# High and low rows side by side in one matmul of 512 columns, in expert jobs of 256 columns

## What is computed

```
def moe(h, router, wg, wu, wd):
    ...
    xs = xf[tok]
    hid = jax.nn.silu(lax.ragged_dot(xs, wg, sizes)) * lax.ragged_dot(xs, wu, sizes)
    ys = lax.ragged_dot(hid, wd, sizes) * gate.reshape(-1)[order][:, None].astype(h.dtype)
    return jnp.zeros_like(xf).at[tok].add(ys).reshape(B, S, D)
```

## Time and profile before

| | |
|---|---|
| Time, median of 3 runs | 4846.22 us (4843.46 to 4847.0) |
| Profiled execution | 4847.46 us, of it 4845.9 us span |
| TensorE matmuls busy in the span | 4269.3 us (88%) |
| VectorE busy in the span | 2434.7 us (50%) |
| ScalarE busy in the span | 1658.1 us (34%) |
| Expert jobs | from about 2480 us to 4778 us |
| VectorE busy in a job of 384 columns, 2733 to 3076 us | 183.07 of 343 us |
| Weights of a tile, 1 MB, from issue to landing | 4.9 us in the median |
| Granted TensorE clock, mean over the span | 0.937 of full |

### The profile page before, as it was taken

One profiled execution on the slowest core, in us unless ns is written; L12 is line 12 of the kernel. 1 busy time (PEld: TensorE's weight loads), 2 busy tenths in 40 slices (PEclk: granted clock), 3 DMA queues, 4 the chain that ended last, 5 costly groups with the idle time before them and its releaser, 6 DMA issues. The chain is left out here.

```text
span 4845.9 us, 66553 instructions
## 1 busy us (share of the span) xinstructions
PE 4269.3 (88%) x23962; PEld 3696.7 (76%) x23963; DVE 2434.7 (50%) x3287; ACT 1658.1 (34%) x2153; POOL 523.0 (11%) x905
## 2 busy tenths in 40 slices
PE   5799999995965688887559999999999999998994
PEld 4688888884864555555459999899999999998993
DVE  3344444452223576652346555566666665554554
ACT  1222222222224466662134333344444444232321
POOL 0000000001122354430120000100000000000001
PEclk9899999996987799998579999999999999999997
DMA  3422232215334211102445433455555554333334
GB/s 115 159 97 95 104 121 95 104 61 179 110 90 155 72 62 51 42 28 98 163 172 184 179 119 128 170 191 198 191 198 191 197 191 178 122 130 136 130 130 178
DMA packets 176461, 643.57 MB, mean 133 GB/s; under 512 B 29936, under 2 KB 68336, under 8 KB 136819
## 3 DMA queue, kind: packets, MB, share of 16 engines
q1 hardware_dynamic: 144452, 540.31, 31.1%
q0 software_dynamic: 20800, 71.87, 3.9%
q10 hardware_dynamic: 11040, 29.36, 1.7%
HBM read 556.88 MB, written 84.59 MB: 132 GB/s over the span
## 5 line engine op out<-in xcount | busy, mean ns | idle before, releaser
L345 PE MATMUL moe_ps<-moe_ht_hi,moe_gu_hi 128*128 128x256 f32 (+1 forms) x3584 | 1085.9, 303 | 24.2 <-issue 19.8
L347 PE MATMUL moe_ps<-moe_ht_hi,moe_gu_lo 128*128 128x256 f32 (+1 forms) x3584 | 1085.0, 303 | 0.0
L346 PE MATMUL moe_ps<-moe_ht_lo,moe_gu_hi 128*128 128x256 f32 (+1 forms) x3584 | 1084.8, 303 | 0.0
L345 PEld LDWEIGHTS moe_ps<-moe_ht_hi,moe_gu_hi 128*128 128x128 f32 x3584 | 683.7, 191 | 30.7 <-issue 25.9
L346 PEld LDWEIGHTS moe_ps<-moe_ht_lo,moe_gu_hi 128*128 128x128 f32 x3584 | 683.8, 191 | 3.8
L347 PEld LDWEIGHTS moe_ps<-moe_ht_hi,moe_gu_lo 128*128 128x128 f32 x3584 | 683.6, 191 | 0.0
L190 ACT CAST moe_gu_hi<-moe_gu_raw 128x2048 fp32r<-128x2048 f32 x226 | 431.4, 1909 | 642.8 <-PE moe_ps L347 520.6
L256 DVE TENSOR_TENSOR moe_gu_lo<-moe_gu_raw,moe_gu_hi 128x2048 fp32r<-128x2048 f32 x226 | 517.3, 2289 | 241.2 <-ACT moe_gu_hi L190 241.2
L286 DVE TENSOR_TENSOR moe_yacc<-moe_yacc,moe_ps 128x512 f32<-128x512 f32 x532 | 362.0, 688 | 378.1 <-PE moe_ps L365 377.4
L363 PE MATMUL moe_ps<-moe_wd_hi,moe_hid_hi 128*128 128x512 f32 x1064 | 415.9, 391 | 0.0
L364 PE MATMUL moe_ps<-moe_wd_lo,moe_hid_hi 128*128 128x512 f32 x1064 | 415.5, 390 | 0.0
(11 more groups left out here) (280 smaller groups left out, 6706.3 us busy)
## 6 DMA issues: line engine op xcount, KB each, us to landing
moe_gu_raw<-in_moe_wgu SPq DMA_DIRECT2D x226, 1024.0 KB, 4.9
moe_wd_raw<-in_moe_wd SPq DMA_DIRECT2D x112, 1024.0 KB
ffn_gu_raw<-in_ffn_wgu SPq DMA_DIRECT2D x58, 1024.0 KB
ffn_wd_raw<-in_ffn_wd SPq DMA_DIRECT2D x28, 1024.0 KB, 5.2
y_moe<-zeros SPq DMA_DIRECT2D x32, 512.0 KB, 3.0
kvq_raw<-in_w_kvq SPq DMA_DIRECT2D x12, 1024.0 KB
qkv<-kvq_o POOLq DMA_DIRECT2D x40, 256.0 KB, 4.9
qt<-heads_qt POOLq DMA_DIRECT2D x16, 512.0 KB, 3.4
```

The costliest lines, as they stand in the source:

```text
L345: pe.matmul(out[:, 0:W], gu_hi[s][:, half, k, :], ht_hi[:, k, 0:W], start=(k == 0), stop=False)
L346: pe.matmul(out[:, 0:W], gu_hi[s][:, half, k, :], ht_lo[:, k, 0:W], start=False, stop=False)
L347: last = pe.matmul(out[:, 0:W], gu_lo[s][:, half, k, :], ht_hi[:, k, 0:W], start=False, stop=(k == KT - 1))
```

## The change

Only jobs of 256 columns change. `ht_hi` and `ht_lo` become two halves of one tile `ht`. A step k of gate or up now has two matmuls in place of three: the high weights run once over 512 columns, the 256 high token columns and the 256 low ones side by side, into the left and the right half of the bank; the low weights run over the 256 high columns into the left half. The value of gate or up is then the sum of both halves. VectorE makes it with a reduction over pairs that lie 256 columns apart: gate into `act_gate`, up into `hid`, each signalled. ScalarE's silu now reads `act_gate`, in SBUF, and waits for the gate sum instead of for TensorE; VectorE's product reads `hid` and waits for silu and for its own up sum. In all other widths VectorE only counts the two new semaphores on.

```
@@ swiglu_jobs @@
-        ht_hi = sb("ht_hi", [P, KT, CAP * P], F32R)
-        ht_lo = sb("ht_lo", [P, KT, CAP * P], F32R)
+        ht = sb("ht", [P, 2, KT, CAP * P], F32R)
+        ht_hi, ht_lo = ht[:, 0, :, :], ht[:, 1, :, :]
...
+        s_gate_sum, s_up_sum = sem("gate_sum"), sem("up_sum")
+
+        def paired(W):
+
+            return 2 * W <= 512
...
                     def silu(N, s):
+                        if paired(W):
+                            act.wait_ge(s_gate_sum, N + 1)
+                            act.activation(act_gate[s][:, 0:W], act_gate[s][:, 0:W], ACT.Silu).then_inc(s_silu, 1)
+                            return
...
                     def product(N, s):
+                        if paired(W):
+                            dve.wait_ge(s_gate, N + 1)
+                            dve.tensor_reduce(act_gate[s][:, 0:W], gate_ps[s][:, 0:2 * W].rearrange("p (a n) -> p n a", a=2),
+                                              AX.X, ALU.add).then_inc(s_gate_sum, 1)
+                            dve.wait_ge(s_gu, N + 3)
+                            dve.tensor_reduce(hid[s][:, 0:W], up_ps[s][:, 0:2 * W].rearrange("p (a n) -> p n a", a=2),
+                                              AX.X, ALU.add).then_inc(s_up_sum, 1)
+                            dve.wait_ge(s_silu, N + 1)
+                            dve.wait_ge(s_up_sum, N + 1)
+                            dve.tensor_tensor(hid[s][:, 0:W], act_gate[s][:, 0:W], hid[s][:, 0:W], ALU.mult).then_inc(s_hid, 1)
+                            return
+                        dve.sem_inc(s_gate_sum, 1)
+                        dve.sem_inc(s_up_sum, 1)
...
                             for k in range(KT):
+                                if paired(W):
+                                    pe.matmul(out[:, 0:2 * W].rearrange("p (a n) -> p a n", a=2), gu_hi[s][:, half, k, :], ht[:, :, k, 0:W],
+                                              start=(k == 0), stop=False)
+                                    last = pe.matmul(out[:, 0:W], gu_lo[s][:, half, k, :], ht_hi[:, k, 0:W],
+                                                     start=False, stop=(k == KT - 1))
+                                    continue
```

## The result

| | before | changed |
|---|---|---|
| Time, median | 4846.6 us (4843.5 to 4853.5) | 4929.4 us (4925.6 to 4937.4) |
| Ratio, 95% interval | | 1.0171 (1.0153 to 1.0189) |
| Profiled execution, its span | 4847.46, 4845.9 us | 4931.15, 4929.6 us |
| First matmul of the experts to the start of the last store of `y_moe` | 2301.1 us | 2390.3 us |
| VectorE busy in the span | 2434.7 us | 2613.9 us |

The change costs 83 us, or 1.7%. It was forecast at +92 us (4939), so sign, size and range came out, but the terms behind it were wrong in opposite directions; that the sum lies so near is luck.

The account below looks back on a forecast made before the run. TensorE was taken as the bound, busy 237.44 of 238 us in a job of 256 columns. The terms -30 + 82 + 22 + 18 = +92 us gave 4939 us, with a range of 4892 to 4972.

Parts of the forecast that it names:

- Part 1, the matmuls: Gate and up on TensorE: a step falls from 0.360 to 0.347 us, 2240 steps, 30 us gained.
- the two blocks: Moving operand of the 512-column matmuls, priced as one block; at 0.013 us more a matmul the 30 us are gone.
- Part 2, the reduction: VectorE's sum over pairs in PSUM: 1.06 us each, bounds 0.69 and 1.43 us.
- L1580 is the nearest row in access pattern: Reason for pricing VectorE's pair reduction at 1.06 us, from a reduction in SBUF jumping 64 elements at each read.
- rival 1: VectorE's reduction costs as a contiguous pass, 0.69 us, giving 4910 us; chance 25%.
- a reduction far from 1.06 us: Sign on VectorE that would show the forecast wrong, its reduction price being 1.06 us.
- steps above 0.35 us a pair: Sign on TensorE that would show the forecast wrong, a gate or up step being priced at 0.347 us.
- Part 3, the odd tiles: Tiles 5, 7 to 27: chain of 6.91 us against 5.55 of cover, TensorE stands 1.36 us, 60 times, 82 us lost.
- Part 4, the starts: First tiles of a job: 6.3 us lost in three jobs, 1.7 in two, together 22 us.
- Part 5, the ends: Before the transposes at a job's end: TensorE stands 4.1 instead of 0.45 us, five jobs, 18 us lost.
- Clock: TensorE's granted clock after pauses at job ends and starts: no loss taken, 14 us kept for the range.
- Loads: Weight loads start some 3 us later at odd tiles but are wanted 17 us later: no cost.

Follow-up runs that it names:

- Experiments 1 to 3: Changed kernel with VectorE's down-block additions behind the odd tile's work: 4868.4 us; with ScalarE's cast ahead of silu: 4867.7 us; with every gate sum made twice: 4981.1 us.
- experiment 9: Changed kernel, but at a job's end VectorE makes four low token tiles ahead of the second last down block's additions: 4915.2 us, 1.0143.
- the last kernel: Changed kernel with additions behind the odd tile, cast ahead of silu, grouped matmuls, four low token tiles ahead of the end additions, per-bank waits: 4835.3 us, 0.9967.
- cast-first kernel: Changed kernel, but ScalarE casts the weights of tile m+2 before it takes silu of tile m: 4867.7 us, 1.0040.
- the reordered one: Changed kernel with both new orders, VectorE's additions behind the odd tile's work and ScalarE's cast ahead of silu: 4858.4 us, 1.0021.
- reordered and grouped kernel: Changed kernel with additions behind the odd tile, cast ahead of silu, and eight matmuls of 512 columns before eight of 256: 4847.9 us, 1.0002.

## Why the prediction was right, and where it was not

**Part 1, the matmuls: mis-sized by half.** The count was right (2240 of each, L368 and L370). The price was put together from rows of matmuls in a run of one width, 0.2267 and 0.120 us, and the steps of a pair in turn don't add up to their sum: 0.3536 instead of 0.347 us. The forecast gain was a difference of 0.013 us, so 0.0066 us more a step halves it. I had named the wrong reason (the two blocks) for the right doubt.

**Part 2, the reduction: wrong value, right bounds.** It costs 0.68 us, the lower bound. The step that failed is "L1580 is the nearest row in access pattern": L1580 jumps in SBUF by 64 elements over 128x1024, and its surcharge does not carry over to pairs in PSUM 256 columns apart. The Trainium skill (SBUF — State Buffer, the note on cachelines under Door 1) gives PSUM lines of 8 bytes, and says that a pattern which is not contiguous slows matmuls; that VectorE's read would be dearer too was my conclusion from it, and the trace doesn't bear it out, 683 ns being the time of a contiguous pass (688). With Part 2 put right and nothing else, rival 1, the forecast would have been 4910 us, 20 too low. The two errors went against one another, 29 us too dear in the reduction and 16 too cheap in the matmuls; and a dearer matmul makes the tile longer that covers the chain, which takes another 6 us off the odd tiles. With all this put right the steps give about 4920 us. What lifts the measured time above that is what I had put at nothing, late loads and the lower clock. So the forecast of 4939 came within 10 us of the measured time by luck: two of the signs that I had named for being wrong, a reduction far from 1.06 us and steps above 0.35 us a pair, both came true.

**Part 3, the odd tiles: right.** Chain and place are as told. With a sum of 0.68 the steps give 6.91 - 0.38 = 6.53 us; 6.35 were found plus the 0.10 of the second matmul (the difference lies in waking TensorE, 0.23 instead of 0.34). Cover 5.65 instead of 5.55. The stall is 0.80 instead of 1.36 us, 48 instead of 82 us. Experiments 1 to 3 show the cause: removed in two ways, it gives the time back; lengthened by 0.60, it costs 52 us.

**Part 4, the starts: right.** VectorE's first sum in the three late jobs comes after 8.5 to 9.1 us of idle time. In the fifth job:

```profile
3623.56 0.69 DVE L279 TENSOR_REDUCE moe_act_gate<-moe_ps 128x256 f32<-128x512 f32 x1 [9.11 <-issue]
...
3631.27 0.68 DVE L279 TENSOR_REDUCE moe_act_gate<-moe_ps 128x256 f32<-128x512 f32 x1
```

```profile
3628.87 0.80 PE L368 MATMUL moe_ps<-moe_ht,moe_gu_hi 128*128 128x512 f32 x1 [4.01 <-DVE moe_gu_lo L265]
3629.46 0.41 PE L370 MATMUL moe_ps<-moe_ht,moe_gu_lo 128*128 128x256 f32 x1
3629.68 0.63 PE L368 MATMUL moe_ps<-moe_ht,moe_gu_hi 128*128 128x512 f32 x1
...
3636.58 0.50 PE L368 MATMUL moe_ps<-moe_ht,moe_gu_hi 128*128 128x512 f32 x1 [0.32 <-DVE moe_gu_lo L265]
```

Tile 2 stands 3.4 to 4.0 us (forecast 3.8). Tile 3 comes 7.71 us later, VectorE's step from sum to sum (3623.56 to 3631.27), against a tile of 5.65: 2.1 us, forecast 2.5. Only 0.32 of it shows as a wait, since the lower clock fills the rest.

**Part 5, the ends: right in the wait.** 3.3 to 3.5 us of wait against 4.1 forecast and 0.45 before; VectorE's queue is its cause (experiment 9). The lower clock comes on top.

**Clock: taken 0, wrong.** The granted clock did fall to its lower level at the job ends (0.71 above), at the three late starts and at tile 5 of three jobs. The 16 transposes after the wait took 3.16 to 3.68 instead of 2.45 us, and behind those of the fourth job the first matmuls stood 0.57 and 0.37 us apart instead of 0.23. At the late starts it costs nothing, as VectorE sets the pace there; at the ends it costs some 7 us and at tile 5, behind the late loads, some 5.5, together near the bound of 14. My reason, "nearer to the row with the short pause", was the weak step: 3.4 us lies between 0.45 and 5.91, and no row told where between them it turns. The Trainium skill (TensorE: Matmul & The Clock Gate, Part 4) says that transposes don't count as work for the clock. The trace agrees in so far as the clock falls with a pause of 3.4 us among transposes, and the 7 us at the ends are near the 9 that the prediction worked out for this rule; but 32 transposes without a pause in the last kernel (4.45 us, granted clock 1.00 from 3554 to 3562 us) did not bring it down.

**Loads: taken 0, wrong.** I wrote that a weight load starts later, but "is wanted 17 us later; it took 4.9 us in the median". That is the steady part of a job. The weights of tile 4 are asked for while the rows of the next job are gathered and the down weights are loaded, and the cast wants them some 5.5 us after their issue. It could begin only 8.6 to 12.7 us after it (the first of the two loads in the first line is that of tile 4):

```profile
3107.28 4.60 SPq L139 DMA_DIRECT2D moe_gu_raw<-in_moe_wgu  x2
3117.05 1.91 ACT L195 CAST moe_gu_hi<-moe_gu_raw 128x2048 fp32r<-128x2048 f32 x1 [4.30 <-DMA moe_gu_raw<-in_moe_wgu]
...
3645.10 1.91 ACT L195 CAST moe_gu_hi<-moe_gu_raw 128x2048 fp32r<-128x2048 f32 x1 [7.19 <-DMA moe_gu_raw<-in_moe_wgu]
```

In the third, fourth, fifth and sixth job (all of 256 columns) this cast waits 4.30, 3.16, 7.19 and 3.15 us. VectorE stands behind it, its four additions and the gate sum of the odd tile come later by as much, and the low weights of tile 5 with them. TensorE then waits 3.08, 1.95, 4.28 and 1.95 us at tile 5, where the other odd tiles wait 0.55, and in the fifth job 1.52 us at tile 4 as well. At tile 5 of three of these jobs the granted clock is down too (0.50 from 3132 to 3136 us). Together that is 16 us, 14 more than before. In the kernel before, this cast waits for its load too (7.2 to 10.0 us), but TensorE loses time only in the third job, 2.5 us: there VectorE begins the low weights of tile 5 0.3 us after the additions, here 3.0 us, behind gate sum, silu and cast. The kernels of experiments 3 and 9, which keep the changed order, show the same long wait at tile 5 of these four jobs (1.8 to 4.6 us), so it is no single event.

## What to carry to other kernels

When an edit puts a new step of engine B ahead of a step of engine A, write out what stands ahead of B's step and what stands behind A's: here a 0.7 us sum behind four additions, with a 1.9 us cast behind it, cost some 90 us where the matmuls gained 14, and moving either neighbour gave most of it back with no instruction fewer. Do not put what frees a buffer behind what waits for a transfer. A load's time in the median says little where several transfers are asked for at once: look at the first tiles of a job by themselves. And when the gain is a small difference of two prices, measure both in the mix in which they will stand.

## What the runs showed of the hardware

- A VectorE reduction over pairs 256 columns apart in one PSUM bank takes 0.683 us for 512 inputs, no more than a contiguous pass (0.688).
- Matmuls of 512 and 256 columns in turn cost 0.3536 us a pair, in groups of eight 0.349, and by the sum of each in a long run 0.347. An operand in one block instead of two makes no difference beyond 0.002 (0.352).
- At the ends of the jobs of 256 columns TensorE pauses between two lots of 16 transposes. With a pause of 3.3 to 3.5 us the granted clock fell at all five (the second lot took 3.16 to 3.68 us instead of 2.45; changed kernel), with 0.9 us at none (experiment 9). With 1.87 us it stayed up at all five in the cast-first kernel and at four of five in the reordered one; with 1.97 us it fell at three of five in the reordered and grouped kernel (2.91 to 3.46 us) and stayed up at two (2.45 us). So with 1.9 to 2.0 us it went either way, and the length of the pause alone doesn't tell. After a pause of 3.38 us at a job start the first pairs still ran at full speed (0.34 and 0.35 us), and the clock fell some 1.4 us after the pause, while TensorE was busy again.
- ScalarE loads a table of 1.28 us ahead of the first silu of a job, and once more when a cast comes ahead of that silu.
- Where a job follows one of the same width, VectorE stands still for 8.5 to 9.3 us ahead of its first instruction, with no releaser that explains it, in the changed kernel and the reordered ones alike (7.9 to 8.2 us before the change), while TensorE runs on without a gap. This wasn't followed up; 9.0 of the 14.1 us that TensorE still waits for low weights in the last kernel stand there.
